# The mLSTM's convolution, queries, keys and gate sums made inside the value-row stage, and its scores with keys in rows

## The reference

```python
proj = h @ w_in[l]
u, vm, z, ipre, fpre, qa, ka, va = jnp.split(proj, offsets, axis=-1)
c = jax.nn.silu(causal_short_conv(u, conv_w[l], conv_b[l]))
qm = jnp.einsum('bshc,hcd->bhsd', ch, wq_m[l])
km = jnp.einsum('bshc,hcd->bhsd', ch, wk_m[l]) * (M_HEAD_DIM ** -0.5)
...
b = jnp.cumsum(jax.nn.log_sigmoid(fpre).reshape(B, H, nc, CHUNK), axis=-1)
c_chunk = jnp.einsum('bhnl,bhnlk,bhnlv->bhnkv', wts, k, v)   # state that a chunk adds
log_d = jnp.where(causal, b[..., :, None] - b[..., None, :] + logi[..., None, :], -jnp.inf)
m_t = jnp.maximum(inter, jnp.max(log_d, axis=-1))
s = jnp.einsum('bhnqd,bhnkd->bhnqk', q, k) * jnp.exp(log_d - m_t[..., None])
num = einsum(s, v) + inter_w[..., None] * einsum(q, C_prev)
den = jnp.sum(s, axis=-1) + inter_w * jnp.einsum('bhnqd,bhnd->bhnq', q, n_prev)
h = num / jnp.maximum(jnp.abs(den), jnp.exp(-m_t))[..., None]
...
hm = rms_norm(hm, mh_norm_g[l]) + skip_m[l] * ch
ym = jax.nn.sigmoid(z) * hm.reshape(B, S, M_WIDTH)
```

## Time and profile before

| | |
|---|---|
| time before, median of 3 runs | 3955.26 us (3951.24 to 3956.1) |
| the profiled execution's own time | 3955.97 us |
| its span | 3954.2 us |
| TensorE, VectorE, ScalarE, GpSimd busy | 92%, 66%, 35%, 35% |
| row stage | 123.5 to 184.1 us |
| `stage_conv` | 184.1 to 206.8 us |
| `stage_mlstm` | 206.8 to 294.7 us |
| dilated attention begins | 294.7 us |

### The profile page before, as it was taken

One profiled execution on the slowest core, in us unless ns is written; L12 is line 12 of the kernel. 1 busy time (PEld: TensorE's weight loads), 2 busy tenths in 40 slices (PEclk: granted clock), 3 DMA queues, 4 the chain that ended last, 5 costly groups with the idle time before them and its releaser, 6 DMA issues. The chain is left out here.

```text
span 3954.2 us, 55713 instructions
## 1 busy us (share of the span) xinstructions
PE 3644.6 (92%) x18894; PEld 2963.3 (75%) x18894; DVE 2622.4 (66%) x5195; ACT 1397.0 (35%) x1968; POOL 1395.4 (35%) x602
## 2 busy tenths in 40 slices
PE   8858989999999979999998999889998988989999
PEld 5645777778888868888886866578887877667877
DVE  7563778888888679999998756485446025745440
ACT  2214223334555422222223137642223133644331
POOL 3003434333333334444442316532222322443443
PEclk9968999999999989999999999999999999999999
DMA  5401444434554666666663463041111214022222
GB/s 207 142 23 53 166 134 141 138 130 153 190 183 160 229 204 191 191 191 193 194 193 125 164 139 53 2 159 64 59 64 45 66 59 117 20 96 99 93 82 87
DMA packets 251694, 494.28 MB, mean 125 GB/s; under 512 B 49283, under 2 KB 129155, under 8 KB 246572
## 3 DMA queue, kind: packets, MB, share of 16 engines
q1 hardware_dynamic: 231100, 452.01, 35.4%
q10 hardware_dynamic: 20480, 40.80, 2.8%
HBM read 411.72 MB, written 73.68 MB: 123 GB/s over the span
## 5 line engine op out<-in xcount | busy, mean ns | idle before, releaser
L426 POOL TENSOR_TENSOR ahead_low<-w_raw,ahead_high 128x1024 fp32r<-128x1024 f32 (+1 forms) x159 | 426.1, 2680 | 888.3 <-ACT ahead_high L362 888.3
L229 PE MATMUL psum<-h_high,ahead_high 128*128 128x512 f32 (+1 forms) x1504 | 539.8, 359 | 3.3 <-POOL ahead_low L426 3.3
L230 PE MATMUL psum<-h_low,ahead_high 128*128 128x512 f32 (+1 forms) x1504 | 540.5, 359 | 0.0
L231 PE MATMUL psum<-h_high,ahead_low 128*128 128x512 f32 (+1 forms) x1504 | 536.7, 357 | 0.0
L1714 POOL TENSOR_TENSOR pick_u_low<-pick_u_raw,pick_u_high 128x1024 fp32r<-128x1024 f32 x128 | 312.8, 2444 | 566.4 <-ACT pick_u_high L1768 566.4
L1972 POOL TENSOR_TENSOR v_low<-v_raw,v_high 128x1024 fp32r<-128x1024 f32 x128 | 308.1, 2407 | 409.6 <-ACT v_high L1956 409.6
L362 ACT ACTIVATE ahead_high<-w_raw 128x1024 fp32r<-128x1024 f32 (+1 forms) x159 | 178.0, 1120 | 744.2 <-PE psum L231 718.6
L229 PE MATMUL psum<-h_high,pick_u_high 128*128 128x512 f32 x1024 | 412.5, 403 | 0.0
L229 PE MATMUL psum<-a_high,v_high 128*128 128x512 f32 x1024 | 399.5, 390 | 13.9 <-DVE v_context L2026 13.9
L230 PE MATMUL psum<-h_low,pick_u_high 128*128 128x512 f32 x1024 | 402.6, 393 | 0.0
L231 PE MATMUL psum<-h_high,pick_u_low 128*128 128x512 f32 x1024 | 399.7, 390 | 0.0
(11 more groups left out here) (396 smaller groups left out, 7435.9 us busy)
## 6 DMA issues: line engine op xcount, KB each, us to landing
pick_u_raw<-in_expert_uT SPq DMA_DIRECT2D x128, 512.0 KB, 3.5
v_raw<-in_expert_v SPq DMA_DIRECT2D x128, 512.0 KB, 3.9
...
gelu_dram<-pick_gelu ACTq DMA_DIRECT2D x128, 256.0 KB, 2.0
...
p<-gelu_dram SPq DMA_DIRECT2D x128, 256.0 KB, 4.8
```

Of the source, the lines that this page charges most:

```text
L229: nc.tensor.matmul(bank, w_high, x_high, start=first, stop=False)
L230: nc.tensor.matmul(bank, w_high, x_low, start=False, stop=False)
L231: return nc.tensor.matmul(bank, w_low, x_high, start=False, stop=last)
L426: nc.gpsimd.tensor_tensor(w_low[r % 2][:, :, :], raw[r % n_raw][:, :, :], w_high[r % 2][:, :, :].bitcast(F32), ALU.subtract).then_inc(k.w_ ...
```

## The change

`stage_conv` is gone. A new object `Cell` stands in `beside` of the row stage, behind the table and the head norms, and does its work at numbered steps:

- VectorE: half a head's convolution at steps 3, 4, 5, 7, 10, 11, 12, 14 (`TAKEN_TAPS`); the gates at 9 and 10; sums, running maxima and scales, now as rows of tokens (16x128), at 13, 16 and 19; weighted key rows at 21 to 23.
- ScalarE: Silu at 5, 8, 12, 15; all copies of queries and keys out of PSUM, a step after their product; the sigmoid at 15; exponentials at 9, 16, 21.
- TensorE: one query or key product at 7, 8, 10, 11, 14, 15, 17, 18 (`QK`), all in bank 5, so that each waits for the copy of the one before; small sums at 11, 14, 17, 20; key rows of three chunks at 20 to 22.

The stage has 5 banks for its jobs instead of 6. The weight columns are in the order gates, mLSTM values, attention values, so the first block ends with the gates, and ScalarE takes a tile in 4, 3 and 1 pieces by block (1, 2 and 2 before). The values go straight into `v_aug`, whose last column is one. The bias table's line is written at step 3, its 8 planes are written from memory to memory at steps 4 to 11, and it is read back at the row stage's end.

`stage_mlstm` keeps only the work on 128x128 tiles. The exponent with keys in rows is summed in PSUM (the causal mask by an identity product of 512 columns, the query's part by four products of 16 rows, `keys`); ScalarE adds the key's part as a bias and takes the exponential per unit (`weigh`); VectorE multiplies by the scores; nothing is transposed before the product with the values. All this goes chunk by chunk, two chunks ahead. Squares and their sums are ScalarE's (`squares`); normalisation, transposing and output go in groups of three chunks and one.

```diff
+def stage_rows(k, w, n_blocks, width, tiles, out, at, beside=(), n_banks=8, step=BANK):
...
+    TAKEN_TAPS = {3: (0, 0), 4: (0, 2), 5: (1, 0), 7: (1, 2), 10: (2, 0), 11: (2, 2), 12: (3, 0), 14: (3, 2)}
+    SILU = {5: 0, 8: 1, 12: 2, 15: 3}
+    QK = {7: 0, 8: 1, 10: 2, 11: 3, 14: 4, 15: 5, 17: 6, 18: 7}
+    ROWS = {20: 0, 21: 1, 22: 2}
...
+        if s - 1 in self.QK:
+            i = self.QK[s - 1]
+            act.wait_ge(self.qk_summed, i + 1)
+            h = i // 2
+            if i % 2 == 0:
+                nc.scalar.activation(self.q_of(h), self.k.psum[:, 5, :], ACT.Copy).then_inc(self.qk_taken, 1)
+            else:
+                nc.scalar.activation(self.kT[:, 2 * h:2 * h + 2, :], self.k.psum[:, 5, :].rearrange("p (a b) -> p a b", b=CTX), ACT.Copy, scale=M_SCALE).then_inc(self.qk_taken, 1)
+        if s in self.SILU:
+            h = self.SILU[s]
+            act.wait_ge(self.conv_done, h + 1)
+            nc.scalar.activation(f.cT[:, h, :], f.cT[:, h, :], ACT.Silu).then_inc(self.c_ready, 1)
+        if s == 15:
+            nc.scalar.activation(f.pT[:, 4:8, :], f.pT[:, 4:8, :], ACT.Sigmoid)
+        if s == 9:
+            nc.scalar.preload_act_table_set("natural_log_exp_and_others")
+            act.wait_ge(self.gates_ready, 1)
+            self.k.act(act, nc.scalar.activation(self.soft[:, :], self.soft[:, :], ACT.Exp))
+            nc.scalar.activation(self.soft[:, :], self.soft[:, :], ACT.Ln, bias=1.0).then_inc(self.soft_ready, 1)
+        if s == 16:
+            nc.scalar.preload_act_table_set("natural_log_exp_and_others")
+            act.wait_ge(self.line_ready, 1)
+            nc.scalar.activation(self.decay_line[:, :], self.decay_line[:, :], ACT.Exp).then_inc(self.decay_ready, 1)
+        if s == 21:
+            act.wait_ge(self.rows_turned, 1)
+            nc.scalar.activation(self.cols[:, 0:3, :].rearrange("p a u -> p (a u)"), self.turned[:, 0:3 * UNITS], ACT.Exp)
+            nc.scalar.activation(self.cols[:, 3, :], self.turned[:, 3 * UNITS:4 * UNITS], ACT.Copy).then_inc(self.cols_ready, 1)
...
+        if s in self.QK:
+            i = self.QK[s]
+            h = i // 2
+            if i == 0:
+                pe.wait_ge(self.w_in, 16)
+            pe.wait_ge(self.c_ready, h + 1)
+            if i:
+                pe.wait_ge(self.qk_taken, i)
+            nc.tensor.matmul(k.psum[:, 5, :], f.w_qk[:, i % 2, h, :], f.cT[:, h, :], start=True, stop=True).then_inc(self.qk_summed, 1)
+        if s == 11:
+            pe.wait_ge(self.lf_ready, 1)
+            nc.tensor.matmul(self.sums_b, self.lf[:, :], k.const("tri"), start=True, stop=True)
+            nc.tensor.matmul(self.sum_line, k.const("ones")[:, 0:1], self.lf[:, :], start=True, stop=True)
+            nc.tensor.matmul(self.sums_li, self.li[:, :], k.const("ident"), start=True, stop=True).then_inc(self.sums_done, 1)
...
+            pe.wait_ge(self.line_ready, 1)
+            nc.tensor.matmul(self.mt_spread[:, 0:1], self.m_line[:, 0:UNITS], one[:, 0:1], start=True, stop=True)
+            nc.tensor.matmul(self.mt_spread[:, 1:2], self.t_line[:, :], one[:, 0:1], start=True, stop=True)
+            pe.wait_ge(self.decay_ready, 1)
+            nc.tensor.matmul(self.decay_spread, one, self.decay_line[:, :], start=True, stop=True).then_inc(self.line_spread, 1)
...
+        if s in self.ROWS:
+            n = self.ROWS[s]
+            if n == 0:
+                pe.wait_ge(self.qk_taken, 2 * M_HEADS)
+            else:
+                pe.wait_ge(self.rows_taken, n)
+            for h in range(M_HEADS):
+                mm = nc.tensor.matmul(k.psum[:, 5, h * P:(h + 1) * P], f.cT[:, h, n * P:(n + 1) * P], f.w_qk[:, 1, h, :], start=True, stop=True)
+            mm.then_inc(self.rows_summed, 1)
...
+        if s in self.TAKEN_TAPS:
+            h, j = self.TAKEN_TAPS[s]
+            u, c = f.pT[:, h, :], f.cT[:, h, :]
+            tap = lambda back: k.par("conv_w", h * 4 + 3 - back)
+            if j == 0:
+                V(dve, nc.vector.tensor_scalar(c, u, tap(0), k.par("conv_b", h), ALU.mult, ALU.add))
+            for back in ((1,) if j == 0 else (2, 3)):
+                ins = nc.vector.scalar_tensor_tensor(c[:, back:SEQ], u[:, 0:SEQ - back], tap(back), c[:, back:SEQ], ALU.mult, ALU.add)
+                if back < 3:
+                    V(dve, ins)
+                else:
+                    ins.then_inc(self.conv_done, 1)
...
+            dve.wait_ge(self.sums_done, 1)
+            V(dve, nc.vector.tensor_copy(self.b_last[:, :], self.sum_line))
+            V(dve, nc.vector.tensor_copy(self.bT[:, :], self.sums_b))
+            V(dve, nc.vector.tensor_tensor(self.rT[:, :], self.sums_li, self.bT[:, :], ALU.subtract))
+            nc.vector.tensor_reduce(self.max_column[:, :], self.rT[:, :], AX_X, ALU.max).then_inc(self.max_ready, 1)
+            V(dve, nc.vector.tensor_tensor_scan(self.runT[:, :], self.rT[:, :], self.rT[:, :], -3e38, ALU.max, ALU.max))
+        if s == 16:
+            dve.wait_ge(self.max_turned, 1)
+            V(dve, nc.vector.tensor_copy(self.r_max[:, :], self.max_line))
+            V(dve, nc.vector.memset(self.m_line[:, 0:M_HEADS], 0.0))
+            for n in range(CHUNKS):
+                now, later = slice(n * M_HEADS, (n + 1) * M_HEADS), slice((n + 1) * M_HEADS, (n + 2) * M_HEADS)
+                V(dve, nc.vector.tensor_tensor(self.t_line[:, now], self.m_line[:, now], self.r_max[:, now], ALU.max))
+                if n < CHUNKS - 1:
+                    V(dve, nc.vector.tensor_tensor(self.m_line[:, later], self.t_line[:, now], self.b_last[:, now], ALU.add))
+            nc.vector.tensor_tensor(self.decay_line[:, :], self.m_line[:, 0:UNITS], self.t_line[:, :], ALU.subtract).then_inc(self.line_ready, 1)
...
+            def keys(n):
+                if n >= 2:
+                    pe.wait_ge(weighted, n - 1)
+                ident = k.const("ident")
+                nc.tensor.matmul(ps[:, spread_bank(n), :], ident, k.const("causal").unsqueeze(1).to_broadcast([P, M_HEADS, P]), start=True, stop=False)
+                for h, u in enumerate(units(n)):
+                    mm = nc.tensor.matmul(ps[:, spread_bank(n), h * P:(h + 1) * P], ident[0:UNITS, u:u + 1].to_broadcast([UNITS, P]), cell.lowT[:, :],
+                                          start=False, stop=(h == M_HEADS - 1))
+                mm.then_inc(spread, 1)
+                if n >= 2:
+                    pe.wait_ge(products_ready, n - 1)
+                for h in range(M_HEADS):
+                    mm = nc.tensor.matmul(ps[:, score_bank(n), h * P:(h + 1) * P], cell.k_of(n, h), cell.q_of(h)[:, tokens(n)], start=True, stop=True)
+                mm.then_inc(scored, 1)
+            def multiply(n):
+                pe.wait_ge(products_ready, n + 1)
+                if n == 0:
+                    pe.wait_ge(states_ready, 2 * M_HEADS)
+                else:
+                    pe.wait_ge(num_taken, n)
+                for h, u in enumerate(units(n)):
+                    mm = nc.tensor.matmul(own(h), sT[:, u, :], f.v_aug[:, u, :], start=True, stop=True)
+                    if n:
+                        mm = nc.tensor.matmul(past(h), cell.q_of(h)[:, tokens(n)], state[:, n - 1, h, :], start=True, stop=True)
+                mm.then_inc(num_summed, 1)
...
+            mm.then_inc(carried, 1)
+            keys(0)
+            keys(1)
+            for n in range(CHUNKS):
+                multiply(n)
+                if n + 2 < CHUNKS:
+                    keys(n + 2)
+            for n in range(CHUNKS):
...
+            def weigh(n):
+                act.wait_ge(spread, n + 1)
+                if n >= 2:
+                    act.wait_ge(num_summed, n - 1)
+                for h, u in enumerate(units(n)):
+                    ins = nc.scalar.activation(sT[:, u, :], ps[:, spread_bank(n), h * P:(h + 1) * P], ACT.Exp, bias=cell.r[:, u:u + 1])
+                ins.then_inc(weighted, 1)
+            def squares(n):
+                act.wait_ge(num_taken, n + 1)
+                for u in units(n):
+                    ins = nc.scalar.activation(square[:, u, :], num[:, u, 0:P], ACT.Square, accum_out=mean[:, u:u + 1])
+                ins.then_inc(squared, 1)
...
+            def take(n):
+                dve.wait_ge(num_summed, n + 1)
+                for h, u in enumerate(units(n)):
+                    ins = nc.vector.tensor_copy(num[:, u, :], own(h))
+                    if n:
+                        V(dve, ins)
+                        ins = nc.vector.scalar_tensor_tensor(num[:, u, :], past(h), cell.inter[:, u:u + 1], num[:, u, :], ALU.mult, ALU.add)
+                ins.then_inc(num_taken, 1)
...
+            product_of(0)
...
+                take(n)
+                if n + 2 < CHUNKS:
+                    product_of(n + 2)
+                if n == CHUNKS - 2:
+                    mean_of(0)
+                    normalise(0)
+            mean_of(1)
+            for n in range(CHUNKS - 1):
+                finish(n)
+            normalise(1)
```

(14 more changed lines are left out.)

508 lines of the change are left out of this document (223 added, 285 removed).

## The result

The changed kernel takes 3896.40 us (median of 4 runs, 3893.34 to 3899.95) against 3955.54 us (4 runs) before: 59 us less, ratio 0.985 with a 95% interval of 0.984 to 0.987. The profiled execution took 3899.95 us, the slowest of the four, so the traces differ by 56.1 us of span (3954.2 to 3898.1) and that is what can be read.

A forecast was written before the change was run, and what follows sets the result against it. TensorE was taken to bound the row stage, hand-overs between engines the mLSTM stage. Row stage 73.6 plus mLSTM 47.5 replace 171.2 us, 50.1 less than the profiled 3955.97: 3905.9, median 3905, range 3893 to 3921.

The forecast's parts named there:

- rival (3): Row and mLSTM stages: full clock and only +8 us in the row stage, 111.5 us together, so 3896; chance 0.08.
- Row stage, products, 11.7 us: Row stage, TensorE: added query, key, key-row and small products cost 6.9, 2.8 and 2.0 us, all on the path.
- New waits, 3.0 us: Row stage: TensorE's new waits at step 8, steps 15 to 17 and step 3 add 3.0 us.
- late weights, 1.3: Row stage, around step 16: late weights stay but cost 1.3 us instead of 2.4, as steps are longer.
- About 2 us are lost: Row stage, steps 15 to 17: ScalarE's chain takes 7.5 us against TensorE's 5.5; half already lost at the copy.
- VectorE, nothing: Row stage: VectorE's convolution and small work counted as nothing; if it falls behind, 1 to 2 us a place.
- Plane writes, 1.25 us, hidden: Row stage, SyncE: each memory-to-memory write of a bias table plane takes 1.25 us, nothing on the path.
- reading back "just hidden": Row stage's end: reading the bias table back takes 9 us, starts when step 23's weights are issued, and is just hidden.
- the walk at full clock, 42.9 us: mLSTM stage: engines' work followed in order at 2.4 GHz, border included, ends at 42.9 us.
- the clock's 4.6 us: mLSTM stage: half-clock spells add 1.7 us early and 2.9 us in later products and transposes, giving 47.5.
- from chunk 1 on it waits 3 to 5 us for each taking, and in such waits the old stage ran at 0.57: mLSTM stage: TensorE's waits for VectorE's takings lower the clock, so later products and transposes at half clock add 2.9 us.
- the rival that stays at half clock: mLSTM stage: half clock throughout, 58.5 us for the stage, 11 us more in all, so 3916; chance 0.16.

The follow-up runs named there:

- the version without the waits at steps 8 to 17: Changed kernel with head norms' factors read one pair a step, two query and key products moved, and the sigmoid at step 13: 3895.23 us, row length 65.8.

## Why the prediction was right, and where its steps were off

It said 3905 in a range of 3893 to 3921; measured 3896. That is below the 3899 to 3911 that had most of the chance (0.58), and it is the time of rival (3), at 0.08, but not by that rival's terms: it had 68.6 and 42.9 us for the two stages, the trace has 74.7 and 41.5. Against the profiled execution it forecast -50.1, and -56.1 came. The stages give the difference: row stage 74.7 for 73.6 (+1.1), mLSTM stage 41.5 for 47.5 (-6.0), the rest 0.7 longer, the border ahead of them 1.8 earlier. The last 3 us to the median are the profiled execution being the slowest of its four. These 3 us and the 1.8 at the border are chance, not part of the change (the first value-row product starts between 123.9 and 127.0 us in the fourteen traces).

- **Row stage, products, 11.7 us.** Right in size: row lengths 67.6 to 71.4 against 56.4 before are +11.2 to +15.0, waits and spells in them; the version without the waits at steps 8 to 17 has +9.4. But before had a wait of 2.36 us and a spell of half clock of its own, some 4 us together, and that version had 0.8 us of wait at step 3, so what was added is about 12.5 us. TensorE's own time sets this stage.
- **New waits, 3.0 us, and late weights, 1.3.** The sum was near, the parts were not. "At step 8 ... TensorE waits some 0.6 us": 0.75 in one unaltered execution, not over 0.29 in the three others. "0.4 us at step 3", for the head norms' squares: none in three of them, 1.08 in the fourth. "About 2 us are lost" at steps 15 to 17: 1.88, and 1.26 to 1.93 in the others, all of it at the copy of step 15 and nothing at step 17. The half that I gave to the copy behind the taking was right and too small; the half that I gave to ScalarE's chain with the sigmoid did not come, and moving the sigmoid left 1.94 us. The late weights were not a term beside it but 0.6 us of the same wait in this execution, and the copy behind the taking the other 1.26; the sigmoid's chain shows once the first wait is gone (2.32 us with the weights late, 0.72 with them in time). Three causes stood one behind another, and only the first in line had a price. That the sum of the parts came near is luck.
- **VectorE, nothing.** Held at the load that the change gives it: no wait for it is in the changed kernel's row stage. It held with little to spare: in the run with 11.3 us more on it TensorE waited for VectorE already at steps 5 and 6.
- **Plane writes, 1.25 us, hidden; reading back "just hidden".** Hidden. In a row a plane took 1.6 us, so the price was somewhat low; even so, writes and reading placed behind all else were late by 1.2 us only.
- **mLSTM stage: the walk at full clock, 42.9 us, was 1.4 too long; the clock's 4.6 us did not come.** The step that failed is "from chunk 1 on it waits 3 to 5 us for each taking, and in such waits the old stage ran at 0.57". There was one such wait, of 2.62 us, and VectorE was busy for 29.3 us and the stage 41.5 us long where the prediction's signs had over 33 and 43 to 58. A `keys` is 3.03 us, not 2.7, and all four lie between the stage's start and product 2, so TensorE, not VectorE, set the pace until 216.5 us and kept its clock; it fell at 220.8 us, so only the last products of chunk 3 and the transposes ran in it, and VectorE waited for none of the first twelve (2.82 us), only for the last four (1.12 us, in its wait of 1.21). Up to the end of taking 2 the walk is within 0.2 us of the trace (21.8 for 22.0 us), with the wrong engine as the pace: takings were shorter (2.4 for 2.9 us), `keys` longer. That agreement is luck. Behind taking 2 the trace is 1.6 us shorter than the walk. Without look-ahead the waits that I had feared were there, 3.3 us each.
- **The rule on the clock.** The Trainium skill (TensorE: Matmul & The Clock Gate, HAM oscillation) would have held the stage at half clock, 58.5 us. The stage here had no bursts with waits between them up to product 3. Entered at half clock it took 3.0 us more; the rival that stays at half clock had 17 more than the trace's 41.5. In the version without look-ahead, 56.0 us at 0.72, the trace agrees with the rule in part: two of its three products behind a wait ran at half clock.

Open: the difference between versions of the row stage in total time, since the rest of the kernel varies by more. Of the new form's 20 us only the look-ahead was tried by itself; what keys in rows, the missing transposes and the chunk-wise outputs give each was not run.
